# Scores of two neighbouring heads on the two row halves of TensorE, the upper head's bank drawn from the weight units' rotation of four

## What is computed

```
h = rmsnorm(x);  q_a,k_a,v_a,q_b,k_b,v_b,z,xbc,dt = split(h @ w_in)
y_a = sliding-window attention with sinks (8 query heads, 2 key heads, head width 64)
y_b = block attention (8 heads of width 64; one block, so causal over 256 tokens)
y_c = Mamba-2 scan with convolution, gated by silu(z)
merged = sum_i sigmoid(h @ w_gate_i) * (y_i @ w_br_i);   x += merged @ w_mix
x += cross-attention;   x += w_down relu(w_up rmsnorm(x))^2
```

## Time and profile before

| | |
|---|---|
| runs | 1233.14 us median of 3 (1230.57 to 1234.44) |
| the profiled execution | 1229.25 us, its span 1227.5 us |
| PE busy | 1183.4 us, 96% of the span |
| PE weight loads | 1085.5 us, 88% |
| DVE busy | 741.4 us, 60% |
| ACT busy | 587.4 us, 48% |
| mean granted TensorE clock | 0.997 of full speed |

### The profile page before, as it was taken

How to read it: one execution, slowest core, us unless ns; L and a number is a source line. 1 busy time by engine, 2 the same in 40 slices (tenths; PEclk the granted TensorE clock), 3 DMA queues, 4 the chain that set the end, 5 groups by cost and what they waited for, 6 DMA issues and landing times.

```text
span 1227.5 us, 19222 instructions
## 1 busy us (share of the span) xinstructions
PE 1183.4 (96%) x8014; PEld 1085.5 (88%) x8014; DVE 741.4 (60%) x1080; ACT 587.4 (48%) x800; POOL 87.3 (7%) x119
## 2 busy tenths in 40 slices
PE   2999999999999999999989999999999999999997
PEld 1998899999898899999879888999999978999996
DVE  3776766685745465555458767568675544645554
ACT  4544544545454354444445554445554444544442
POOL 4000001420000000000020000023100000000000
PEclk9999999999999999999999999999999999999999
DMA  6652534547654446555627444266556453555561
GB/s 154 202 167 75 181 123 140 174 150 258 192 167 133 144 158 200 183 196 171 206 84 228 137 138 135 81 180 217 179 180 198 138 171 104 205 187 191 182 211 38
DMA packets 155424, 201.37 MB, mean 164 GB/s; under 512 B 6097, under 2 KB 110921, under 8 KB 155337
## 3 DMA queue, kind: packets, MB, share of 16 engines
q1 hardware_dynamic: 155208, 200.08, 50.1%
q0 software_dynamic: 128, 0.06, 0.3%
HBM read 199.04 MB, written 1.08 MB: 163 GB/s over the span
## 4 chain that ended last, share of the span: by engine, by line
PE 87%; DVE 4%; ACT 3%; issue 2%; POOL 2%; DMA 2%; SPq 1%; DVEq 0%; POOLq 0%; ACTq 0%
PE psum L1041 15%; PE psum L1042 15%; PE psum L1043 15%; PE psum L1050 10%; PE psum L1052 10%; PE psum L1051 10%; PE psum L1114 2%; PE psum L1155 2%; PE psum L1127 1%; PE psum L1200 1%; PE psum L1177 1%; DMA raw<-in_w_br_moba_dram 1%; PE psum L1085 1%; POOL sms L693 1%; DVE w_lo L1344 1%
## 5 line engine op out<-in xcount | busy, mean ns | idle before, releaser
L1344 DVE TENSOR_TENSOR w_lo<-raw,w_hi 128x2048 fp32r<-128x2048 f32 (+1 forms) x184 | 418.7, 2278 | 267.4 <-ACT w_hi L721 267.4
L721 ACT ACTIVATE w_hi<-raw 128x2048 fp32r<-128x2048 f32 (+2 forms) x188 | 349.2, 1858 | 153.6 <-PE psum L1052 130.9
L1041 PE MATMUL psum<-act_hi,w_hi 128*128 128x256 f32 x1344 | 385.3, 287 | 0.0
L1043 PE MATMUL psum<-act_hi,w_lo 128*128 128x256 f32 x1344 | 380.1, 283 | 0.0
L1042 PE MATMUL psum<-act_lo,w_hi 128*128 128x256 f32 x1344 | 380.1, 283 | 0.0
L1041 PEld LDWEIGHTS psum<-act_hi,w_hi 128*128 128x128 f32 x1344 | 257.6, 192 | 1.9 <-issue 0.5
L1042 PEld LDWEIGHTS psum<-act_lo,w_hi 128*128 128x128 f32 x1344 | 257.7, 192 | 1.1 <-issue 0.5
L1043 PEld LDWEIGHTS psum<-act_hi,w_lo 128*128 128x128 f32 x1344 | 257.5, 192 | 0.0
L1050 PE MATMUL psum<-w_hi,relu_hi 128*128 128x512 f32 x256 | 99.8, 390 | 0.0
L1051 PE MATMUL psum<-w_lo,relu_hi 128*128 128x512 f32 x256 | 99.8, 390 | 0.0
L1052 PE MATMUL psum<-w_hi,relu_lo 128*128 128x512 f32 x256 | 99.6, 389 | 0.0
(11 more groups left out here) (245 smaller groups left out, 1788.9 us busy)
## 6 DMA issues: line engine op xcount, KB each, us to landing
raw<-in_w_in_dram SPq DMA_DIRECT2D x36, 1024.0 KB, 5.2
raw<-in_w_up_dram SPq DMA_DIRECT2D x32, 1024.0 KB, 5.4
raw<-in_w_down_dram SPq DMA_DIRECT2D x32, 1024.0 KB, 5.1
raw<-in_w_gate_dram SPq DMA_DIRECT2D x24, 1024.0 KB, 7.1
raw<-in_w_ckv_dram SPq DMA_DIRECT2D x16, 1024.0 KB, 5.3
raw<-in_w_br_ssd_dram SPq DMA_DIRECT2D x8, 1024.0 KB, 9.6
raw<-in_w_mix_out_dram SPq DMA_DIRECT2D x8, 1024.0 KB, 5.1
raw<-in_w_cq_dram SPq DMA_DIRECT2D x8, 1024.0 KB, 5.1
```

The source lines that it names most:

```text
L721: ins = act.activation(w_hi[:, slot, cut], raw[:, slot, cut], ACT.Copy)
L1041: pe.matmul(dst, m_hi[:, k, cs], a_hi[:, k, :], start=k == 0, stop=False)
L1043: ins = pe.matmul(dst, m_lo[:, k, cs], a_hi[:, k, :], start=False, stop=k == kt - 1)
L1344: dve.tensor_tensor(w_lo[:, slot, 0:n], raw[:, slot, 0:n], w_hi[:, slot, 0:n].bitcast(F32), ALU.subtract).then_inc(lo_ready.sem, 1)
```

## The change

A job's two heads were `4*(j//2) + j%2` and that plus 2. Both lie on the same half of the 128 partitions, and their scores went into one bank. Now they are heads `2j` and `2j+1`, which lie on the lower and on the upper 64 partitions of one tile, so the two matmuls use different row halves of the array. The lower head keeps bank 4. The upper head's scores get a bank of their own out of the units' rotation: `IN_TURN` takes `turn % 4` and moves `turn` on by one, in the order of the slots. PE waits for both banks ahead of the two matmuls, each matmul signals its own bank full, DVE waits for both and frees each after its own mask instruction. A step counter between DVE's mask and its maxima is gone, since the two bank releases now say the same. The number of instructions on PE is the same.

```
 def head_of(j, i):
-    return 4 * (j // 2) + j % 2 + 2 * i
+    return 2 * j + i
...
+IN_TURN = -1
...
     if 0 <= job_at(s) < SSD_JOB0:
-        out.append((SB_, ("score", job_at(s))))
+        out += [(SB_, ("score", job_at(s), 0)), (IN_TURN, ("score", job_at(s), 1))]
...
         for bank, key in slot_banks(u):
+            if bank == IN_TURN:
+                bank = turn % 4
+                turn += 1
             use(bank, key)
...
             def job_scores(l, n):
...
-                pe.wait_ge(*is_free(l, key))
+                for i in range(2):
+                    pe.wait_ge(*is_free(l, ("score", n, i)))
                 qk = (qkT_a, qkT_b)[branch]
-                half_p = slice((j % 2) * HD, (j % 2 + 1) * HD)
+                k_tile = 4 + (j // 2 if branch == 0 else j)
                 for i in range(2):
-                    q_tile = head_of(j, i) // 2
-                    k_tile = 4 + (j // 2 if branch == 0 else q_tile)
-                    ins = pe.matmul(bank(key)[:, i * 2 * P:i * 2 * P + (t + 1) * P],
-                                    qk[half_p, q_tile, t * P:(t + 1) * P], qk[half_p, k_tile, 0:(t + 1) * P],
-                                    start=True, stop=True)
-                ins.then_inc(full(key), 1)
+                    key = ("score", n, i)
+                    half_p = slice(i * HD, (i + 1) * HD)
+                    pe.matmul(bank(key)[:, 0:(t + 1) * P], qk[half_p, j, t * P:(t + 1) * P],
+                              qk[half_p, k_tile, 0:(t + 1) * P], start=True, stop=True).then_inc(full(key), 1)
...
             def job_mask(l, n):
...
-                    dve.wait_ge(*is_full(l, key))
+                    for i in range(2):
+                        dve.wait_ge(*is_full(l, ("score", n, i)))
...
-                    if i == 0:
-                        steps.mark(ins)
-                ins.then_inc(free(key), 1)
-                steps.settle()
-                dve.wait_ge(*is_read(l, key))
...
+                    dve.tensor_tensor_reduce(s_sb[:, n % 2, c:c + keys], bank(key)[:, 0:keys], mask, 1.0,
+                                             -3.0e38, ALU.add, ALU.max, row_max[:, i:i + 1]).then_inc(free(key), 1)
+                for i in range(2):
+                    dve.wait_ge(*is_read(l, ("score", n, i)))
```

More of the change, by code:

```diff
@@ L1102, in job_scores @@
                 branch, t, j = job_of(n)
-                key = ("score", n)
                 if n == 0:
@@ L1582, in job_mask @@
                 for i in range(2):
-                    c = i * 2 * P
-                    ins = dve.tensor_tensor_reduce(s_sb[:, n % 2, c:c + keys], bank(key)[:, c:c + keys], mask, 1.0,
-                                                   -3.0e38, ALU.add, ALU.max, row_max[:, i:i + 1])
-                    if i == 0:
-                        steps.mark(ins)
-                ins.then_inc(free(key), 1)
-                steps.settle()
-                dve.wait_ge(*is_read(l, key))
+                    c, key = i * 2 * P, ("score", n, i)
+                    dve.tensor_tensor_reduce(s_sb[:, n % 2, c:c + keys], bank(key)[:, 0:keys], mask, 1.0,
+                                             -3.0e38, ALU.add, ALU.max, row_max[:, i:i + 1]).then_inc(free(key), 1)
+                for i in range(2):
+                    dve.wait_ge(*is_read(l, ("score", n, i)))
                 if branch == 0:
                     c = PC_SINK + head_of(j, 0)
-                    steps.link(dve.tensor_tensor(row_max[:], row_max[:], par[:, c:c + 3:2], ALU.max))
+                    steps.link(dve.tensor_tensor(row_max[:], row_max[:], par[:, c:c + 2], ALU.max))
                 h = HEADS * t + head_of(j, 0)
-                dve.tensor_scalar(neg_max[:, branch, h:h + 3:2], row_max[:], -ATT_SCALE, None, ALU.mult)\
+                dve.tensor_scalar(neg_max[:, branch, h:h + 2], row_max[:], -ATT_SCALE, None, ALU.mult)\
                    .then_inc(masked.sem, 1)
```

## The result

The changed kernel takes 1241.89 us (median of 6, 1239.4 to 1244.15), the kernel before beside it 1231.28 us (median of 6). The ratio is 1.0089, with a 95% interval of 1.0076 to 1.0103: 10.6 us slower. The profiled execution took 1244.15 us, with a span of 1242.4 us (14.9 us more than before) and a mean granted clock of 0.990. It is the slowest of the six.

The account below looks back on a forecast made before the run. PE's matmul queue was taken as the bound. 1229.25 - 5.0 (pairs) + 15.9 (stalls) + 2.2 (clock) = 1242.3 us profiled, 13.1 more than before; on the median 1233.14 that gives 1246 us, range 1238 to 1254.

Parts of the forecast that it names:

- the three stalls: PE waits for just-filled banks at units 14, 17, 20: 1.4, 4.55, 2.0 us a layer, 15.9 us for both layers.
- The pairs: Score matmuls on PE: two heads' four passes take the time of three, saving 5.0 us; bounds 0 and 10.0 us.
- rival 1: Score matmuls: halves work fully side by side, saving 10.0 us, and the clock holds; 1239 us, chance 0.13.
- The clock: PE drops to half clock after unit 17's stall, 0 to 1.6 us each, taken as 1.1, 2.2 us for both layers.
- the halves don't overlap: Score matmuls: no overlap of row halves, and the clock falls fully at each unit 17; 1252 us, chance 0.15.
- stalls come back: Other engines get ahead while PE stands, recovering up to 5.1 us of `y_tok` waits; 1241 us, chance 0.07.
- The other side: DVE's slot 16: `z` leaves its bank before unit 17 wants it, only the saving stays; 1228 us, chance 0.05.

Follow-up runs that it names:

- chosen banks: Changed kernel, but the upper score takes a bank used by neither neighbouring unit, without moving the units' rotation: 1221.63 us, ratio 0.9922 against the kernel before.
- the doubled pairs: Kernel with chosen banks, every pair of score matmuls issued twice: 1232.03 us, ratio 1.001 against the kernel before.
- the filler: Changed kernel, with 18 unused matmuls of 512 columns issued by PE just before unit 17: 1238.82 us, ratio 1.0073 against the kernel before.
- the old pairs: Changed kernel, with a job's heads again on the same row half, the upper scores' bank still from the moving rotation: 1251.35 us, ratio 1.0167 against before.
- only unit 17: Kernel with chosen banks, where only the upper scores of jobs 8 and 9 move the rotation on: 1234.21 us, ratio 1.004 against the kernel before.
- the `z` products first: Changed kernel, with DVE's first `z` stripe products moved ahead of the turned-x products and the close in slot 16: 1232.41 us, ratio 1.0013 against before.

## Why the prediction came out as it did

**Direction and place: right.** PE's queue is the bound, and the three stalls stand where the prediction put them, in both layers, with the releasers it named. With chosen banks they vanish and the kernel is faster than before.

**The stalls: 15.9 us predicted, 16.5 found.** Counted from the start of the last piece ahead to the unit's start, units 14, 17 and 20 lose 1.50, 4.65 and 2.10 us more than before (1.4, 4.55 and 2.0 predicted). The rest is 0.1 us in each of the six, the time from a release to PE's start. The prediction took 0.05 us, read where ACT releases PE behind `y_tok`. Behind DVE's `z` it is 0.15 us, and it is as long where ACT releases a bank, at unit 14:

```profile
110.48 1.08 ACT L760 ACTIVATE v_b<-psum 128x512 f32<-128x512 f32 x2
...
111.22 0.36 PE L1045 MATMUL psum<-act_hi,w_hi 128*128 128x256 f32 x1 [1.26 <-ACT v_b L760]
```

The first copy's record is 0.60 us long and ends at 111.08, 0.14 us ahead of PE's start. Why `y_tok` is quicker is open.

**The pairs: mis-sized.** The step was that a head's second pass "can't run beside its first, but the upper head's first can run beside the lower head's second. If the halves work side by side and matmuls start in program order, four passes take the time of three", 5.0 us. The four passes start two by two, and the pairs save 10.1 us. On the same half they follow each other (1.05 us, each head in its own bank), so the two that start together must be of different heads. That was the size in rival 1; the doubled pairs and the overlap of the starts decide it. The Trainium skill's sentence on parallel tiles (TensorEngine Tiling (Array Packing), Key Properties) made it 10.0 us, and the trace agrees. What the prediction drew from program order doesn't hold here. Whether the passes are queued as lower, upper, lower, upper or whether one overtakes another can't be seen in these records, which don't say which head a pass belongs to.

**The clock: right in kind, too small.** 2.2 us were summed for unit 17 (1.1 for each drop, 1.6 at most). 2.6 us are in the changed kernel's profile, and 2 to 3 us come back with the filler. But in the profile of the old pairs the same wait was followed by 2.0 and 2.4 us of loss, and in that of only unit 17 by 1.4 and 2.0, so the bound of 1.6 was too low. The prediction counted unit 20 out, but its wait of 1.85 us was followed by a lower clock in the second layer. In this profile the clock was also low at two places where no bank changed hands, near 31 and 847 us, where before it was full. Both follow a wait of PE that is there before as well, 1.93 us for `h_tok` (1.77 before) and 1.71 us for `y_tok` (1.29 before). The stretches of the changed kernel:

```profile
770.10:775.10 5.00, 5.00 (x29) 5.00 (x30) 2.72 (x2) 2.30 (x5) 0.00 (x0) 0.66 0.09 6
28.00:36.00 8.00, 6.07 (x25) 4.88 (x24) 2.85 (x9) 5.12 (x10) 1.49 (x3) 0.79 0.21 52
845.00:852.00 7.00, 5.86 (x37) 5.86 (x38) 4.30 (x8) 4.91 (x9) 2.46 (x3) 0.76 0.50 164
```

So a wait of this length is sometimes followed by half the clock and sometimes not: that of unit 20, always 1.85 us, was in three of its eight cases in four profiles (the changed kernel, the old pairs, the `z` products first, the filler). What decides it is open. The changed kernel's runs stray with the granted clock, from 1239.4 us at 0.994 to 1244.15 us at 0.990.

**The next wait: left out.** Faster pairs bring PE earlier to the exponentials, 0.8 us more in the list of waits.

The sum with the sizes found: 16.5 - 10.1 + 2.6 + 0.8 = 9.8 us, and up to 1.5 us more where unit 20 loses clock too, against 10.6 measured between the medians. In the profiled execution the low clock at unit 20 and at 31 and 847 us comes on top, and its span is 14.9 us longer. The prediction's +13.1 us was 2.5 too high against the medians: the pairs took off 5.1 more than thought, stalls, clock and exponentials put 1.8 back, and the remaining 0.8 is not traced to one place. These errors have opposite signs, so that the sum came as close as it did is in part luck. The forecast of 1246 us lies 4 us above the 1241.89 measured, since the kernel before, too, came out 1.9 us lower over six runs (1231.28) than over the three that the forecast starts from (1233.14).

**The other rivals.** That the halves don't overlap is excluded by the pairs. That stalls come back is excluded by the kernel with only unit 17. The other side (no wait at the units) is what the chosen banks make; it was not what this rotation does.

Not tried: both heads on two halves into one bank. The Trainium skill (TensorEngine Tiling (Array Packing), Restrictions and Gotchas) says that different row tiles can't access the same bank at once; no run here shows it.

## What to carry to other kernels

When a new tenant enters a rotation of buffers, write down for each user who held its buffer before and whether that one can be empty yet; here the extra turns met stripes that held two buffers over two slots, and the unit behind each got a buffer just filled. A saving on the engine that bounds the kernel and a wait on it have the same price, so compare them in us: 10 against 19 to 21 here, clock included. Keep two half-height matmuls next to each other in the queue, or the second half brings nothing.

## What was not expected of the hardware

Two float32 matmuls with a contraction of 64, on different row halves and next to each other, took 0.42 and 0.64 us (128 and 256 columns) instead of 0.64 and 1.05. One alone took 0.63 us with 256 columns, as much as the pair. And standing for 4.4 us cost TensorE 1.2 to 2.4 us beyond the wait (six cases in three profiles), which matmuls that compute nothing of use could avoid. Waits of 1.7 to 1.95 us were followed by half the clock in some cases and not in others.
